# A hybrid decoder step: the first pair of expert blocks gathered before the last row tile is routed, its rows added by products with a selection matrix

## Chip, cores and metric

One core of a Trainium2 chip runs the whole program as one launch. The metric is the device time of that launch in microseconds.

## What is computed

One trunk layer for 512 prompt tokens and 8 samples, 520 rows of 1024, all in fp32. A mixer (pooling and a state-space scan) is followed by the output projection and a residual. Then comes the part that matters here, a mixture of 32 experts, cut to its core:

```python
def _hier_moe(u, ...):
    t = u.reshape(n * L, d)                      # u = rmsnorm(h)
    g_w, g_idx = lax.top_k(softmax(t @ rg_w + rg_b), 1)      # one group of 4
    e_w, e_idx = lax.top_k(softmax(e_sel), 2)                # two of its 8 experts
    hg = einsum('td,edf->tef', t, w_gate[g]); hu = einsum('td,edf->tef', t, w_up[g])
    act = silu(hg) * hu * gate[:, :, None]
    out = out + einsum('tef,efd->td', act, w_down[g])
```

After it come a gated per-layer input and a last norm. Each token has two experts, 1040 choices in all.

## The kernel before

The kernel is written engine by engine; the order on each engine is written out by hand, and semaphores join them. Names: `pe` is TensorE, `dve` VectorE, `act` ScalarE, `pool` GpSimd, `sp` SyncE, which only issues DMA.

**Row tiles.** The 520 rows are five tiles, taken in the order `ORDER = [0, 1, 4, 2, 3]` (tile 4 holds the 8 samples, tile 3 comes last). For each, `out_half` makes the output projection, `residual` (VectorE) adds it into `h1`, `half_square` and `inverse_root` make 1/rms on ScalarE and GpSimd, and `store_row` (ScalarE) writes the normed rows to the DRAM buffer `u_dram`. In parallel `h_rows` transposes h, `take_h` copies it with the gain, `route` makes the router's logits, and on VectorE `take_logits`, `choose` and `rank` pick two experts for each row (one-hot in `oh`) and the row's place among the rows of its expert; the count behind `rank` is a product (`count`) of triangular and full ones with the choices so far. `rank` leaves `posh`, for each row the one-hot of its place times its token number.

**Blocks.** An expert's rows fill a block of 64 places; two blocks make a pair of 128. `fill_slots(i)` multiplies `posh` by the choices and sums, over all five tiles, the table of row numbers for the 16 pairs of the first 32 blocks (bank PS[1]); VectorE turns it into `out_all` and `idx_all`. A place with no row keeps the number EMPTY and falls out of the gather's bounds, so G, cleared before, holds zeros there. `fill_extra_slots` does the same for blocks beyond the first 32.

**The hand-over.** GpSimd waits for the table and for all five stores of `u_dram`, then gathers pairs 0 and 1 into the two halves of `G` (an indirect DMA each). `pair_rows` transposes G's rows by TensorE, four tiles for each half of the 1024 features, and `take_pair` copies them with the gain to `uT`. Every later pair is gathered two pairs ahead.

**The expert blocks.** Block b on TensorE: `gate_up` (16 products for gate and up from `uT`), `down` of block b-1, half a pair's `pair_rows`, then `act_rows`, which transposes the activations. ScalarE makes silu, VectorE `gate_act`, `take_pair` and `take_act`. The first 24 blocks are written out (`HEAD`), the rest are a loop whose length VectorE computes (`extra_blocks`). SyncE loads 3 MB of weights for each block; there are seven buffers for gate and up and five for down. Those of blocks 0, 1, 3 and 6 are loaded early, those of 2, 4 and 5 when the output projection is done, and block b+7 when `gate_up(b)` is done:

```python
for b in range(HEAD):
    if b >= 1:
        ...
        sp.wait_ge(s_Y_ready, b)          # down(b - 1) done
        load_down(dn_slot(nxt), bass.ds(nxt, 1))
    if b + NGU < HEAD + U:
        sp.wait_ge(s_up_done, b + 1)      # gate_up(b) done
        load_gate_up(gu_slot(b + NGU), bass.ds(b + NGU, 1))
```

Behind the blocks come the scatter of the last rows, their loads by token, the gate of the per-layer input and the last norm.

Of the kernel before, what the change touches and what calls it, by code (L numbers as in the profile page):

```python
# [12 lines left out]
BF16 = mybir.dt.bfloat16  # L13
I32 = mybir.dt.int32
U32 = mybir.dt.uint32
ALU = mybir.AluOpType
# [88 lines left out]
def build(nc, a, o):  # L105
    ctx = ExitStack()
    with ctx:
# [77 lines left out]
        junk = at(R_g, D)  # L185
        spool = at(R_act, PW, rows=NS * BUF)
# [189 lines left out]
        s_slot_ready = sem("s_slot_ready")  # L376
        s_pos_ready = sem("s_pos_ready")
# [87 lines left out]
        def _(sp):  # L465
# [28 lines left out]
            sp.dma_start(o["conv_s"][0, :, 0:2, :], a["state_conv"][0, :, 1:3, :]).then_inc(st_shift, 16)  # L494

# [90 lines left out]
            sp.wait_ge(st_shift, 32)  # L586
# [4 lines left out]
        def _(pe):  # L591
# [314 lines left out]
            def fill_slots(i):  # L906

                pe.wait_ge(s_pos_ready, i + 1)
                for k in range(2):
                    j = 2 * ORDER[i] + k  # L910
                    choice = oh[:, ORDER[i], k * NE:(k + 1) * NE].rearrange("p (b q) -> p q b", q=2)
                    for q in range(2):
                        ins = pe.matmul(PS[1][q * S:(q + 1) * S, 0:MAIN], posh[:, j, :], choice[:, q, :],
                                        start=(i == 0 and k == 0), stop=(i == NT - 1 and k == 1))
# [3 lines left out]
            def fill_extra_slots():  # L918
                pe.wait_ge(s_slot_ready, 1)
                for j in range(2 * NT):  # L920
                    for q in range(2):
                        ins = pe.matmul(PS[3][q * S:(q + 1) * S, MAIN:NP_], posh[:, j, :],
                                        blkx[:, j, :].rearrange("p (b q) -> p q b", q=2)[:, q, :],
                                        start=(j == 0), stop=(j == 2 * NT - 1))
                ins.then_inc(s_tab_done, 1)
# [181 lines left out]
        def _(act):  # L1107
# [144 lines left out]
            def half_square(i, h):  # L1252
# [3 lines left out]
                squares = A(junk[0:R, h * 512:(h + 1) * 512], h1[0:R, t, h * 512:(h + 1) * 512], ACT.Square, scale=root_d,  # L1256
# [8 lines left out]
            def store_row(i):  # L1265
# [6 lines left out]
                act.wait_ge(s_u_ready, i + 1)  # L1272
                act.dma_start(u_dram[t * P:t * P + R, :], row[0:R, i % 2, :]).then_inc(u_stored[i % 2], 16)
# [22 lines left out]
            for b in range(HEAD):  # L1296
                act.wait_ge(s_up_done, b + 1)
                silu_gate(b)
                if b >= 1:
                    act.wait_ge(s_Y_ready, b)  # L1300
                    if b % 2 and b >= 5:
                        act.wait_ge(y_written[(b // 2) % 2], 16 * (b // 4))
# [87 lines left out]
        def _(pool):  # L1390
# [71 lines left out]
            pool.wait_ge(st_fin, 16)  # L1462
            for i in range(NT):
# [23 lines left out]
            for p in range(2):  # L1487
                gather(p, idx_all[:, p:p + 1])
# [40 lines left out]
        def _(dve):  # L1529
# [228 lines left out]
            def rank(i):  # L1758
# [7 lines left out]
                for k in range(2):  # L1766
# [4 lines left out]

            residual(0, 0)
# [35 lines left out]
            residual(4, 1)  # L1808
            take_h(4, 1)
# [3 lines left out]

            dve.wait_ge(s_tab_done, 1)
            step(ts(out_all[:, 0:MAIN], PS[1][:, 0:MAIN], float(EMPTY), None, ALU.add))
            ts(idx_all[:, 0:MAIN], out_all[:, 0:MAIN], 1, None, ALU.arith_shift_right).then_inc(s_tab_ready, 1)

            step(tt(ex4, L[:, :, 0:4], gmax[:, :, 0:1].to_broadcast((P, NT, 4)), ALU.subtract))
            tt(e21, ev[:, :, 1], ev[:, :, 0], ALU.subtract).then_inc(s_rt_a, 1)

# [12 lines left out]
            step(dve.tensor_copy(rank_i, rk))  # L1833
            step(ts(rank_i, rank_i, 6, None, ALU.arith_shift_right))
            step(dve.tensor_copy(rq, rank_i))
            step(stt(rr, rq, -float(S), rk, ALU.mult, ALU.add))

            step(ts(cmp0, rq, 0.5, None, ALU.is_gt))
            step(tt(ovt, ovt, rq, ALU.add))
            step(tt(ovt, ovt, cmp0, ALU.mult))  # L1840
            step(ts(ovt, ovt, -1.0, None, ALU.add))

            tt(posh, iota_s.unsqueeze(1).to_broadcast((P, 2 * NT, S)),
               rr.rearrange("p t k -> p (t k)").unsqueeze(2).to_broadcast((P, 2 * NT, S)), ALU.is_equal)
            step(tt(blkx, iota_s[:, 0:NBX].unsqueeze(1).to_broadcast((P, 2 * NT, NBX)),
                    ovt.rearrange("p t k -> p (t k)").unsqueeze(2).to_broadcast((P, 2 * NT, NBX)), ALU.is_equal))
            tt(blkx, blkx, const[:, C_TOKID:C_TOKID + 2 * NT].unsqueeze(2).to_broadcast((P, 2 * NT, NBX)), ALU.mult
               ).then_inc(s_slot_ready, 1)

            dve.wait_ge(s_rt_b, 1)  # L1850
            step(dve.tensor_reduce(gw, ex4, AX.X, ALU.add))
            step(stt(gw, e21, 1.0, gw, ALU.add, ALU.mult))
            step(dve.reciprocal(wgt[:, :, 0], gw))
            step(tt(wgt[:, :, 1], wgt[:, :, 0], e21, ALU.mult))

            def extra_blocks():
                dve.wait_ge(s_tab_done, 2)
# [16 lines left out]
            def take_pair(slot, half):  # L1874
                tt(uT[:, slot, half * 512:half * 512 + 512].rearrange("p (k c) -> p k c", c=P), tiles(PS[6 + half][:, :]),  # L1875
# [177 lines left out]
```

## Time and profile before

| | |
|---|---|
| median of 3 runs | 575.98 us (574.41 to 576.43) |
| the profiled execution: its time, its span | 574.31 us, 572.5 us |
| TensorE busy, share of the span | 509.9 us, 89% |
| VectorE, ScalarE, GpSimd busy | 207.7, 153.7, 110.7 us |
| bytes moved by DMA, mean rate | 144.72 MB, 253 GB/s |
| mean granted TensorE clock | 0.961 |

A fp32 product is recorded as two instructions, a transpose as one. The hand-over lies at 218 to 249 us of the span, the expert blocks from there to 488, the tail behind them. The share of busy time is a mean over stages with different limits; which wait ends last has to be read stage by stage.

### The profile page before, as it was taken

What the parts mean: (1) busy time and instruction counts of PE and PEld (TensorE: products, weight loads), DVE (VectorE), ACT (ScalarE), POOL (GpSimd) and SP (SyncE); (2) the same over time, 40 slices, a digit from 0 to 9 for tenths busy, and PEclk for the clock granted to TensorE, in tenths of its full rate; (3) what the DMA queues carried; (4) which work ended last, traced back from release to release, by engine and by line L of the source; (5) the groups of instructions that cost most, each with busy time, mean ns of one, the idle gap of its engine ahead of it and who ended that gap; (6) DMA issues with size and microseconds to landing.
All of it is one profiled execution on the core that took longest, in us unless ns stands there. A gap on an engine that the chain in (4) does not pass through costs nothing.

```text
span 572.5 us, 7815 instructions
## 1 busy us (share of the span) xinstructions
PE 509.9 (89%) x3098; PEld 313.3 (55%) x3098; DVE 207.7 (36%) x496; ACT 153.7 (27%) x315; POOL 110.7 (19%) x178
## 2 busy tenths in 40 slices
PE   5899999999999995299999999978849999799994
PEld 4788886768645553255555555534424553344443
DVE  1285696322034456431112221111111110467455
ACT  0435263113424022012222222221111223433224
POOL 1200059991001001201111111101111222111001
PEclk9999999999999998589999999998987999899998
DMA  8990002303359506849999999999999998700001
GB/s 289 417 291 2 1 1 73 149 1 89 147 243 395 246 37 258 330 174 393 419 416 415 414 416 417 415 416 418 416 406 384 410 412 344 306 2 2 38 37 73
DMA packets 40214, 144.72 MB, mean 253 GB/s; under 512 B 14522, under 2 KB 15162, under 8 KB 31076
## 3 DMA queue, kind: packets, MB, share of 16 engines
q1 hardware_dynamic: 33316, 132.79, 58.6%
q0 software_dynamic: 5152, 8.85, 4.2%
q10 hardware_dynamic: 1712, 2.62, 1.2%
q8 instruction: 23, 0.38, 0.3%
q14 instruction: 11, 0.09, 0.0%
HBM read 140.15 MB, written 14.19 MB: 270 GB/s over the span
## 4 chain that ended last, share of the span: by engine, by line
PE 45%; DMA 10%; DVE 3%; issue 2%; ACT 1%; SPq 0%; POOL 0%; POOLq 0%; DVEq 0%; ACTq 0%
PE PS L989 18%; PE PS L1091 10%; PE PS L1010 10%; DMA mem<-in_exp_w_down 5%; PE PS L593 4%; DVE mem L1875 2%; DMA u_rows<-mem 2%; DMA mem<-u_rows,idx_all 1%; DMA choice_rows<-mem,out_i 1%; PE PS L834 1%; PE PS L935 1%; PE PS L990 1%; DMA mem<-choice_rows 1%; DVE mem L1917 1%; PE PS L996 1%
## 5 line engine op out<-in xcount | busy, mean ns | idle before, releaser
L989 PE MATMUL PS<-mem 128*64 128x256 f32 x512 | 119.6, 387 | 6.8 <-DVE mem L1875 6.8
L990 PE MATMUL PS<-mem 128*64 128x256 f32 x512 | 119.6, 387 | 0.0
L989 PEld LDWEIGHTS PS<-mem 128*64 128x64 f32 x512 | 68.6, 139 | 43.3 <-DVE mem L1875 7.6
L1010 PE MATMUL PS<-mem 128*64 128x512 f32 x256 | 64.2, 624 | 16.8 <-DMA mem<-in_exp_w_down 8.6
L633 PE MATMUL PS<-mem 128*128 128x260 f32 x320 | 73.3, 385 | 0.0
L990 PEld LDWEIGHTS PS<-mem 128*64 128x64 f32 x512 | 68.6, 139 | 0.0
L633 PEld LDWEIGHTS PS<-mem 128*128 128x128 f32 x320 | 59.8, 190 | 10.5 <-issue 1.5
L593 PEld LDWEIGHTS PS<-mem 128*128 128x128 f32 (+4 forms) x254 | 31.7, 172 | 47.8 <-issue 30.6
L1879 DVE TENSOR_TENSOR mem<-PS,mem 64x256 f32<-64x256 f32 x32 | 13.7, 427 | 120.0 <-ACT mem L1288 120.0
L821 PE MATMUL PS<-mem 128*128 128x512 f32 x128 | 56.6, 595 | 0.0
L1091 PE MATMUL PS<-mem 128*128 128x512 f32 (+1 forms) x144 | 55.6, 545 | 0.0
L593 PE MATMUL PS<-mem 128*128 128x128 f32 (+4 forms) x254 | 40.6, 292 | 14.7 <-DMA mem<-u_rows,idx_all 12.4
L1875 DVE TENSOR_TENSOR mem<-PS,mem 128x512 f32<-128x512 f32 x34 | 23.5, 692 | 75.4 <-PE PS L593 75.2
L1288 ACT ACTIVATE mem<-PS 64x256 f32<-64x256 f32 x32 | 12.0, 376 | 134.8 <-PE PS L990 134.8
L1010 PEld LDWEIGHTS PS<-mem 128*64 128x64 f32 x256 | 18.8, 141 | 42.6 <-issue 30.6
L1091 PEld LDWEIGHTS PS<-mem 128*128 128x128 f32 x144 | 27.1, 190 | 26.6 <-issue 25.8
L1402 POOL TENSOR_TENSOR mem<-mem 128x1 f32<-128x1 f32 (+1 forms) x20 | 4.1, 207 | 182.0 <-ACT mem L1256 85.1
L821 PEld LDWEIGHTS PS<-mem 128*128 128x128 f32 x128 | 23.8, 190 | 26.9 <-issue 26.8
L604 PE MATMUL PS<-mem 128*128 128x260 f32 x128 | 31.3, 410 | 6.9 <-DMA mem<-in_w_a 6.9
L1293 ACT ACTIVATE mem<-PS 64x512 f32<-64x512 f32 x32 | 18.9, 591 | 65.4 <-PE PS L1010 65.4
L604 PEld LDWEIGHTS PS<-mem 128*128 128x128 f32 x128 | 26.1, 205 | 11.3 <-DMA mem<-in_w_a 6.9
L1480 POOL DMA_INDIRECT mem<-u_rows,idx_all x15 | 15.3, 1022 | 81.5 <-PE PS L593 72.6
(270 smaller groups left out, 546.8 us busy)
## 6 DMA issues: line engine op xcount, KB each, us to landing
mem<-in_exp_w_down SPq DMA_DIRECT2D x32, 1024.0 KB, 21.2
mem<-in_exp_w_gate SPq DMA_DIRECT2D x32, 1024.0 KB, 18.7
mem<-in_exp_w_up SPq DMA_DIRECT2D x32, 1024.0 KB, 21.9
mem<-in_w_out SPq DMA_DIRECT2D x2, 2048.0 KB, 7.5
mem<-in_ple_gate_w SPq DMA_DIRECT2D x1, 4096.0 KB, 29.6
mem<-choice_rows SPq DMA_DIRECT2D x4, 1024.0 KB, 8.4
mem<-in_xT SPq DMA_DIRECT2D x4, 520.0 KB, 9.1
mem<-in_w_a SPq DMA_DIRECT2D x4, 512.0 KB, 9.9
```

The source lines that it names most:

```text
L593: return pe.transpose(dst, src, ident[0:n, 0:n])
L604: ins = pe.matmul(PS[A_BANKS[j][h]][:, 0:HALF], COLS[j][2][:, k, :], xg[k // 4][:, k % 4, h * HALF:(h + 1) * HALF], start=(k == 0), stop=( ...
L633: ins = pe.matmul(PS[b + h][:, 0:HALF], w[:, k, :], aT[:, k, h * HALF:(h + 1) * HALF], start=(k == 0), stop=(k == KT - 1))
L821: return pe.matmul(PS[OUT_BANKS[i][h]][:, :], mix_col(k, ORDER[i]), w_out[:, k, h * 512:(h + 1) * 512], start=(k == 0), stop=(k == KT - 1))
L989: pe.matmul(PS[0][0:S, 0:FF], rows_k, gu[slot][:, k, :], start=(k == 0), stop=(k == KT - 1))
L990: ins = pe.matmul(PS[1][S:2 * S, 0:FF], rows_k, gu[slot][:, KT + k, :], start=(k == 0), stop=(k == KT - 1))
L1010: ins = pe.matmul(PS[4 + h][h * S:(h + 1) * S, :], actT[:, s % 2, f * S:(f + 1) * S], dn[slot][:, f, h * 512:(h + 1) * 512], start=(f == 0 ...
L1091: ins = pe.matmul(PS[4 if q else 2 * (i % 2) + h][:, 0:w], uTr[:, i % 2, k * P:(k + 1) * P], w_ple[:, k, h * 512 + q * w:h * 512 + (q + 1) ...
L1293: A(ysb[rows, s // 2, 0:512], PS[4][0:S, :], ACT.Copy)
L1480: pool.indirect_dma_start(G[:, q, :], None, u_dram, bass.IndirectOffsetOnAxis(ap=idx, axis=0), bounds_check=TOK - 1, oob_is_err=False).the ...
L1875: tt(uT[:, slot, half * 512:half * 512 + 512].rearrange("p (k c) -> p k c", c=P), tiles(PS[6 + half][:, :]), g_ffn[:, 4 * half:4 * half + ...
L1879: tt(act_tok[:, s % 2, :], PS[1][S:2 * S, 0:FF], sg[:, s % 2, :], ALU.mult).then_inc(s_act_ready, 1)
```

## The change

The table of the first pair is summed once more, apart, over the first four tiles in order (`first_pair_slots`, two columns, PS[1]), and pair 0 is gathered from it as soon as these four tiles are stored. Rows of the last tile (tile 3) are missing in G then, and stay zero there. VectorE builds from the last tile's ranks and choices a selection matrix `sel` of 128 rows by 128 places, with the row's 1/rms as its value (`first_pair_rows`). TensorE sums, in two cleared banks, eight products of G's rows with the identity and eight of the raw `h1` of the last tile with `sel` (`first_pair`); the sum is what the transposed rows were. The full table moves to PS[3] and is made afterwards; pair 1 is gathered with it, once its half of G, where `sel` and its parts are kept until then, has been cleared.

The extra slots, both halves of pair 1's transposes and `extra_blocks` move behind the down product of block 0, in block 1's turn; VectorE's `extra_choices` (overflow ranks and weights) moves behind block 0's gate. ScalarE squares into another scratch (`junk_h`). The DRAM rows of the last tile are first filled with a copy of `x_prompt`, issued early on SyncE, the last store waits for it.

```diff
+            sp.dma_start(u_dram[tl * P:(tl + 1) * P, :], a["x_prompt"][0, tl * P:(tl + 1) * P, :]).then_inc(st_shift, 16)
...
+            SEL = [PS[0], PS[2]]
+            def first_pair_zero():
+                pe.wait_ge(s_outp_out, 9)
+                for half in range(2):
+                    pe.matmul(SEL[half][:, :], bef[:, 0:1].to_broadcast((P, P)), const[:, 0:256].bitcast(BF16),
+                              start=True, stop=False)
+            def first_pair(rows, place, half, last_part):
+                for q in range(4):
+                    ins = pe.matmul(SEL[half][:, q * P:(q + 1) * P], rows.rearrange("s (p k) -> s k p", k=KT)[:, 4 * half + q, :],
+                                    place, start=False, stop=last_part and q == 3)
+                if last_part:
+                    ins.then_inc(s_T_done, 1)
+            def first_pair_slots():
+                pe.wait_ge(s_pos_ready, NT - 1)
+                for i in range(NT - 1):
+                    for k in range(2):
+                        t = ORDER[i]
+                        choice = oh[:, t, k * NE:(k + 1) * NE].rearrange("p (b q) -> p q b", q=2)
+                        for q in range(2):
+                            ins = pe.matmul(PS[1][q * S:(q + 1) * S, 0:2], posh[:, 2 * t + k, :], choice[:, q, 0:2],
+                                            start=(i == 0 and k == 0), stop=(i == NT - 2 and k == 1))
                 ins.then_inc(s_tab_done, 1)
...
             out_half(4, 1, 6, KT)
+            first_pair_slots()
             h_rows(4, 1)
             route(4)
+            first_pair_zero()
             for i in range(NT - 1):
                 fill_slots(i)
             count(4)
+            pe.wait_ge(g_full[0], 16)
+            for half in range(2):
+                first_pair(G[:, 0, :], ident, half, False)
+            pe.wait_ge(s_sel_ready, 1)
+            for half in range(2):
+                first_pair(h1[:, ORDER[NT - 1], :], sel, half, True)
             fill_slots(4)
             count_all()
...
-            pe.wait_ge(g_full[0], 16)
-            pe.wait_ge(s_lg_out, NT)
-            pair_rows(0, 0)
-            pe.wait_ge(s_cnt_taken, 1)
-            pair_rows(0, 1)
-            fill_extra_slots()
...
-                if b % 2 == 0:
-                    pe.wait_ge(g_full[(b // 2 + 1) % 2], 16 * ((b // 2 + 1) // 2 + 1))
-                pair_rows((b // 2 + 1) % 2, b % 2)
+                if b == 1:
+                    pe.wait_ge(g_full[1], 16)
+                    pe.wait_ge(s_lg_out, NT)
+                    pe.wait_ge(s_cnt_taken, 1)
+                    pair_rows(1, 0)
+                    pair_rows(1, 1)
+                    fill_extra_slots()
+                elif b >= 2:
+                    if b % 2 == 0:
+                        pe.wait_ge(g_full[(b // 2 + 1) % 2], 16 * ((b // 2 + 1) // 2 + 1))
+                    pair_rows((b // 2 + 1) % 2, b % 2)
...
             pool.wait_ge(st_fin, 16)
+            step(pool.memset(G[:, 0, :], 0.0))
...
-            step(pool.memset(G, 0.0))
-
-            pool.wait_ge(s_tab_ready, 1)
-            pool.wait_ge(u_stored[0], 48)
-            pool.wait_ge(u_stored[1], 32)
...
-            for p in range(2):
-                gather(p, idx_all[:, p:p + 1])
+            pool.wait_ge(s_tab_ready, 1)
+            pool.wait_ge(u_stored[0], 32)
+            pool.wait_ge(u_stored[1], 32)
+            pool.wait_ge(st_shift, 48)
+            gather(0, idx_i[0][:, 0:1])
+            pool.wait_ge(s_T_done, 2)
+            step(pool.memset(G[:, 1, :], 0.0))
+            pool.wait_ge(s_tab_ready, 2)
+            pool.wait_ge(u_stored[0], 48)
+            gather(1, idx_all[:, 1:2])
...
+            def first_pair_rows(i):
+                t = ORDER[i]
+                R = ROWS[t]
+                step(tt(hit[0:R], iota_s[0:R, :].unsqueeze(1).to_broadcast((R, 2, S)),
+                        rk[0:R, t, :].unsqueeze(2).to_broadcast((R, 2, S)), ALU.is_equal))
+                for k in range(2):
+                    ins = stt(selk[0:R, k], hit[0:R, k].unsqueeze(1).to_broadcast((R, 2, S)), rstd[0:R, 5 + t:6 + t],
+                              oh[0:R, t, k * NE:k * NE + 2].unsqueeze(2).to_broadcast((R, 2, S)), ALU.mult, ALU.mult)
+                step(ins)
+                tt(sel[0:R, :].rearrange("p (q s) -> p q s", s=S), selk[0:R, 0], selk[0:R, 1], ALU.add).then_inc(s_sel_ready, 1)
...
             residual(4, 1)
+            dve.wait_ge(s_tab_done, 1)
+            step(ts(out_i[0][:, :], PS[1][:, 0:1], float(EMPTY), None, ALU.add))
+            ts(idx_i[0][:, :], out_i[0][:, :], 1, None, ALU.arith_shift_right).then_inc(s_tab_ready, 1)
             take_h(4, 1)
             take_logits(4)
             choose(4)
             rank(4)
...
+            first_pair_rows(4)
...
+            for half in range(2):
+                dve.wait_ge(s_T_done, half + 1)
+                take_rows_of(PS[2 * half], 0, half)
+
+            dve.wait_ge(s_tab_done, 2)
...
             for b in range(HEAD):
                 dve.wait_ge(s_sg_ready, b + 1)
                 gate_act(b)
-                dve.wait_ge(s_T_done, b + 3)
-                take_pair((b // 2 + 1) % 2, b % 2)
+                if b == 0:
+                    extra_choices()
+                else:
+                    for n in (range(2) if b == 1 else range(b % 2, b % 2 + 1)):
+                        dve.wait_ge(s_T_done, 2 * (b // 2) + 3 + n)
+                        take_pair((b // 2 + 1) % 2, n)
                 dve.wait_ge(s_actT_done, b + 1)
                 take_act(b)
-                if b == 0:
+                if b == 1:
                     extra_blocks()
```

## Rows read from the trace of the kernel before

**Rows 1.** The chain that ended last, 215 to 262: start us, us, what.

```profile
221.63 8.84 DMA u_rows<-mem
...
231.50 7.76 DMA mem<-u_rows,idx_all
...
239.30 1.97 PE PS L593 x8
...
241.27 2.25 PE PS L922 x40
...
244.03 0.42 PE PS L989
...
249.34 0.39 ACT mem L1288
```

**Rows 2.** Timeline of TensorE: start us, us, engine, line, tiles, shapes, count.

```profile
210.06 1.88 PE L886 MATMUL PS<-mem 128*128 128x40 f32 x16
...
216.02 1.96 PE L821 MATMUL PS<-mem 128*128 128x512 f32 x4
...
218.76 0.66 PE L593 MATMUL PS<-mem 128*128 128x128 f32 x4 [0.78 <-DVE mem L1710]
...
221.29 1.11 PE L913 MATMUL PS<-mem 128*64 128x16 f32 x32
...
239.30 1.97 PE L593 MATMUL PS<-mem 128*128 128x128 f32 x8 [12.45 <-DMA mem<-u_rows,idx_all]
```

**Rows 3.** Stretches: length, busy of each engine, then TensorE clock, DMA share, GB/s.

```profile
220.00:224.00 4.00, 2.37 (x43) 2.10 (x42) 2.40 (x14) 1.15 (x1) 2.12 (x2) 1.00 1.00 412
...
240.00:244.00 4.00, 4.00 (x50) 3.48 (x51) 1.38 (x2) 0.00 (x0) 0.99 (x1) 0.50 0.16 43
...
248.00:252.00 4.00, 3.70 (x32) 2.34 (x30) 2.15 (x7) 0.38 (x1) 0.00 (x0) 1.00 0.35 109
...
424.00:428.00 4.00, 0.00 (x0) 0.00 (x0) 0.00 (x0) 0.00 (x0) 0.00 (x0) 0.69 0.99 396
```

**Rows 4.** Timeline of SyncE's queue, its DMA issues.

```profile
39.81 0.64 SPq L494 DMA_DIRECT2D out_conv_s<-in_state_conv  x1
...
249.34 0.33 SPq L484 DMA_DIRECT2D mem<-in_exp_w_gate  x1
...
255.93 0.38 SPq L490 DMA_DIRECT2D mem<-in_exp_w_down  x1
```

**Rows 5.** Waits of TensorE, 360 to 480: in total, times, longest.

```profile
PE PS L1010 <- DMA mem<-in_exp_w_down: 8.6, 2, 7.4
```

**Rows 6.** Timeline of VectorE, 226 to 234.

```profile
226.65 0.17 DVE L1815 TENSOR_SCALAR out_all<-PS 128x16 int32<-128x16 f32 x1 [0.71 <-PE PS L913]
...
228.79 0.49 DVE L1831 TENSOR_TENSOR mem<-mem 128x320 f32<-128x320 f32 x1
...
229.85 0.17 DVE L1833 CAST int_w<-mem 128x10 int32<-128x10 f32 x1
...
233.65 0.17 DVE L1854 TENSOR_TENSOR mem<-mem 128x5 f32<-128x5 f32 x1
```

**Rows 7.** Timeline of GpSimd, ahead of the first gather.

```profile
220.31 1.80 POOL L1467 MEMSET mem<- 128x2048 f32 x1
```

**Rows 8.** Single transfers, by line: one load of weights (L490), one gather (L1480).

```profile
L490 SPq DMA_DIRECT2D mem<-in_exp_w_down x1: 447/447/447, 221.0 to 221.0; - x1
...
DMA to landing us min/median/max: 21.0/21.0/21.0
...
L1480 POOL DMA_INDIRECT mem<-u_rows,idx_all x1: 988/988/988, 242.0 to 242.0; - x1
...
DMA to landing us min/median/max: 3.9/3.9/3.9
```

**Rows 9.** Stretches around TensorE's restart at 430, columns as in rows 3.

```profile
430.00:432.00 2.00, 1.67 (x4) 0.53 (x6) 0.00 (x0) 0.00 (x0) 0.00 (x0) 0.50 0.89 363
...
435.00:436.00 1.00, 1.00 (x7) 0.93 (x8) 0.69 (x1) 0.34 (x1) 0.44 (x3) 0.63 1.00 336
```

More of the change, by code:

```diff
@@ L185, in build @@
         junk = at(R_g, D)
+        junk_h = at(R_g + D, D)
+        sel = at(R_g + D, 2 * S)
+        selk = at(R_g + D + 2 * S, 2, 2, S)
+        hit = at(R_g + D + 6 * S, 2, S)
         spool = at(R_act, PW, rows=NS * BUF)
@@ L376, in build @@
         s_slot_ready = sem("s_slot_ready")
+        s_sel_ready = sem("s_sel_ready")
         s_pos_ready = sem("s_pos_ready")
@@ L912, in fill_slots @@
                     for q in range(2):
-                        ins = pe.matmul(PS[1][q * S:(q + 1) * S, 0:MAIN], posh[:, j, :], choice[:, q, :],
+                        ins = pe.matmul(PS[3][q * S:(q + 1) * S, 0:MAIN], posh[:, j, :], choice[:, q, :],
                                         start=(i == 0 and k == 0), stop=(i == NT - 1 and k == 1))
@@ L1272, in store_row @@
                 act.wait_ge(s_u_ready, i + 1)
+                if i == NT - 1:
+                    act.wait_ge(st_shift, 48)
                 act.dma_start(u_dram[t * P:t * P + R, :], row[0:R, i % 2, :]).then_inc(u_stored[i % 2], 16)
@@ L1300, in _ @@
                     act.wait_ge(s_Y_ready, b)
+                    if b == 1:
+                        act.wait_ge(u_stored[0], 48)
+                        act.wait_ge(u_stored[1], 32)
                     if b % 2 and b >= 5:
@@ L1812, in _, with take_rows_of @@
             rank(4)
-            dve.wait_ge(s_tab_done, 1)
-            step(ts(out_all[:, 0:MAIN], PS[1][:, 0:MAIN], float(EMPTY), None, ALU.add))
-            ts(idx_all[:, 0:MAIN], out_all[:, 0:MAIN], 1, None, ALU.arith_shift_right).then_inc(s_tab_ready, 1)
+            first_pair_rows(4)
             step(tt(ex4, L[:, :, 0:4], gmax[:, :, 0:1].to_broadcast((P, NT, 4)), ALU.subtract))
             tt(e21, ev[:, :, 1], ev[:, :, 0], ALU.subtract).then_inc(s_rt_a, 1)
+            def take_rows_of(bank, slot, half):
+                tt(uT[:, slot, half * 512:half * 512 + 512].rearrange("p (k c) -> p k c", c=P), tiles(bank[:, :]),
+                   g_ffn[:, 4 * half:4 * half + 4].unsqueeze(2).to_broadcast((P, 4, P)), ALU.mult).then_inc(s_uT_ready, 1)
+            for half in range(2):
+                dve.wait_ge(s_T_done, half + 1)
+                take_rows_of(PS[2 * half], 0, half)
+            dve.wait_ge(s_tab_done, 2)
+            step(ts(out_all[:, 0:MAIN], PS[3][:, 0:MAIN], float(EMPTY), None, ALU.add))
+            ts(idx_all[:, 0:MAIN], out_all[:, 0:MAIN], 1, None, ALU.arith_shift_right).then_inc(s_tab_ready, 1)
             oh4 = oh.rearrange("p t (k e) -> p (t k) e", e=NE)
@@ L1843, in _ @@
[L1843 to L1848, printed above, removed]
@@ L1874, in take_pair @@
             def take_pair(slot, half):
-                tt(uT[:, slot, half * 512:half * 512 + 512].rearrange("p (k c) -> p k c", c=P), tiles(PS[6 + half][:, :]),
-                   g_ffn[:, 4 * half:4 * half + 4].unsqueeze(2).to_broadcast((P, 4, P)), ALU.mult).then_inc(s_uT_ready, 1)
+                take_rows_of(PS[6 + half], slot, half)
             def gate_act(s):
@@ L1882, in take_act @@
                 dve.tensor_copy(actT[:, s % 2, :], PS[2][:, 0:2 * S]).then_inc(s_actT_ready, 1)
-            for half in range(2):
-                dve.wait_ge(s_T_done, half + 1)
-                take_pair(0, half)
             for b in range(HEAD):
```

42 lines of the change are left out of this document (26 added, 16 removed).

## The prediction

> **What bounds the kernel now.** I read the chain that ended last first, around the hand-over from routing to the expert blocks. From 221.63 to 249.3 us it is one string of five pieces: the store of the last row tile (8.84 us), the gather of the first pair of blocks (7.76), eight transposes of its rows (1.97), the extra-slot products (2.25), then the sixteen gate/up products of block 0, 5.8 us up to ScalarE's first gate at 249.34 [rows 1]. TensorE has nothing to do from 226.84 to 239.30 [rows 2].
>
> Next the stage behind it, since a gain here is worth only what the block stage lets through. The windows show the weight stream: the prefetch of blocks 2, 4 and 5 fills the DMA engines until about 240, then their share is 0.16 at 240 to 244, still 0.35 at 248 to 252, and behind that, but for one short gap, about 1.0, as still at 424 to 428 [rows 3]. SyncE can refill no slot before block 0's products end: refill A goes out at 249.34, refill B waits for block 0's down product and goes out at 255.93 [rows 4]. Past 360, the down products wait 8.6 us for their weights in the records, and longer than that in all [rows 5]. So the blocks are bound by the weight stream, and the stream's start is set by the end of block 0. What brings that end forward brings the whole stream forward, as long as it falls into the idle stretch 240 to 250. The stages behind the blocks then follow rigidly.
>
> **The change part by part.** I compare when block 0's gate/up products end: 249.3 before.
>
> *The gather leaves earlier.* It left at 231.50, 1.03 us after the store of the last tile landed [rows 1]. Now it needs the slot table of four tiles only. The last out projection products end at 217.98; 16 small products for 2 columns cost what the 16 for 16 columns did (32 instructions, 1.11 us) [rows 2], and the two VectorE conversions take 0.38 (0.17 each and the gap, [rows 6]), so the table is there at 219.6. GpSimd comes later: its fifth inverse root ends as the 1.80 us clearing of G starts, at 220.3, and that clearing is gone (half to before the roots, where GpSimd idles, half to behind the sums) [rows 7]. With the idle step and an issue of some 0.7 us: 221.1, **10.4 us earlier**. The stores it waits for are long done.
>
> *How long it takes.* It starts as the 7 MB prefetch fills the queues; the last of its seven loads goes out at 221.04 [rows 8]. Near rows: 7.76 us for this gather, 8.84 for the store issued at 221.63, both beside the prefetch [rows 1]; 3.9 for a gather at 242.04 on quiet DMA [rows 8]. Full queues are the nearer case: 7.8 us, it lands at 228.9. **0**, with ends -3.9 and +1.1. The Trainium skill, "DMA: Bandwidth & Descriptors", section "Anatomy of one DMA — SWDGE (gpsimd) path", fits 2.0 us plus bytes / 436e3 per microsecond for a DMA from GpSimd; for some 65 rows of 4 KB that gives an estimate of 2.6 us. Both loaded rows here disagree threefold; by the fit the sum would be some 4 us better (the quick-gather rival).
>
> *Sixteen products for eight transposes.* A transpose is one instruction, an fp32 product two. At full clock four transposes take 0.66 us and 16 instructions of 128x128 weights with 40 columns 1.88, each with the tail of the last [rows 2]: about 0.11 us apiece, so I price a product of 128 columns at two of those. At half clock it is 0.22: double that, and the eight transposes in 1.97 with the tail of the last agree [rows 1]. The clock was at half, 1.2 of 2.4 GHz, after TensorE's idle time, at 240 to 244 [rows 3], and will be again, since TensorE is idle from some 225.2 to 228.9. When it took up dense products at 430.33 after a wait (busy 1.67 of the first two us), the clock was back within the slice 435 to 436, 5.3 us later [rows 9]. So of 32 x 0.22 = 7.0 us, 5.3 run at half and the rest in 0.85; with 0.15 for the tail, 6.3 us: **4.3 more** than the 1.97. Bounds: all at full 3.7, all at half 7.2.
>
> The Trainium skill, "TensorE: Matmul & The Clock Gate", section "Terms", calls the transpose mode four times faster for fp32. No row here has a transpose and a product of the same 128 columns side by side; by this rule a product would cost four transposes and sixteen of them 14.1 us (a rival below).
>
> *The selection matrix must not be late.* The table products delay the last transposes of h by 0.35 us (218.76 to 219.1, [rows 2]), the conversions fit before them, so the last rank ends at 226.3 instead of 225.94. Four VectorE operations of 128 elements follow; between 0.17 for 16 and 0.49 for 320 [rows 6] I put 0.28 each, 1.25 with gaps: ready at 227.5. It is wanted only after the first eight products, at some 232.4. Cost **0**; the cover is 5 us. The two clearing products (bf16, 512 columns, some 0.5 us in all) lie in TensorE's wait for the last choice.
>
> *Between products and block 0.* The 2.25 us of extra-slot products leave the path. In their place stands VectorE's last copy, 0.85 with its start; the last slot fill and the total count (some 0.9 together at half clock) lie beside it. **-1.4**. They return behind block 1's down product at full clock, some 1.35 us.
>
> *Block 0 at full clock.* Before, the clock was back only for the slice from 248 [rows 3], with a pair of products every 0.42 us until then [rows 1]. Now it starts 7 us after TensorE resumed, at full clock, 3.6 us: **-2.2**, with 0 as the other end.
>
> *Block 0's down product.* VectorE now works out the overflow (4.0 us, 229.85 to 233.82 in [rows 6]) between block 0's gate and the copy of its activation. Gate/up of block 1 (3.6) covers most; 0.35 us of wait is left: **+0.35**. The second gather can't leave until G's second half, which holds the matrix, is cleared: 0.9 us after the sums, at about 237; at 7.8 us it lands at 245, before the down product ends at 246.6. A tail of only 1.6 us, so I give it +0.5 in the range. Queued behind that wait are both row transposes of pair 1, the extra slots and block 1's activation, so block 2 and refill C.
>
> *The stream.* A moves by -9.7, B by -9.35, block 2 by only some -7.5 (both halves of pair 1 and the extra slots now sit in front of it). B to C grows from 6.8 to 8 us; B's 3.1 MB and two row transfers need about 8.2, so at most a gap of some 0.2 opens. Behind that the stream is full and the 1.9 us by which TensorE lags is taken from its own waits past 360. The 0.5 MB copy in DRAM is issued on SyncE at 40.5, behind the copy at 39.81, where SyncE has nothing else to issue for long after [rows 4]: 0. ScalarE's added waits find their transfers done. The other scratch area costs nothing.
>
> Sum: -10.4 + 0 + 4.3 - 1.4 - 2.2 + 0.35 + 0.2 = **-9.2 us**. Against the profiled execution's 574.31 that is 565.1; that execution is 1.7 below the median of the runs, so against 575.98 it is **566.8**. A change under 0.5% (2.9 us) can't be told from none here.
>
> **The rivals.**
> *The clock stays low.* If all products run at half, 0.9 is lost; if block 0 does too (sixteen pairs at 0.42, [rows 1]), 3.2 more: 567.7 to 570.9. For it: before, TensorE worked from 239.3 and the clock was back only at 248 [rows 3]. Against: most of that was transposes and 12-column products; the dense ones began at 243.5.
>
> *Quick gather.* It leaves two or three microseconds into the prefetch and takes the 3.9 us of quiet DMA [rows 8]: lands at 225, the first eight products are done when the matrix comes, the sums end 3.7 earlier, 563.1. Against: the share is 1.00 from 220 on [rows 3].
>
> *Products at four times a transpose.* 14.1 for 6.3 us: -1.4 remains, 575.4 with the clock as above; no measurable change.
>
> *The stream hides it.* If the blocks are bound by bytes and the idle share at 240 to 252 isn't usable, TensorE only waits longer past 360: 576. Against it, refill A starts the stream within 2 us.
>
> *Slower: the gather is held in the burst.* It now shares the engines with the prefetch's start, no longer with its end. If its rows come through only as the burst drains, it lands when the last prefetch does, 21.0 us after that one's issue at 221.04 [rows 8], at 242.0. That is 13.1 later than I count: +3.9, 579.9. It decides from a landing at 238.1 on, where the 9.2 are used up. Against: the store issued at 221.63 beside the same burst took 8.84.
>
> **How the numbers follow.** As summed 0.50 (own range 564.5 to 568.5); clock stays low 0.20; quick gather 0.10; four-fold products 0.05; stream hides it 0.06; held gather 0.06; 0.03 for something else on the good side. Faster by over 0.5%: 0.83, within 0.11, slower 0.06. The range must hold 8 in 10: from just under the quick gather, 563.0, to the low clock with 1.3 us of bounds on the gather, 572.5.
>
> **What would show it.** Right: first gather leaves at 221 to 222 and lands near 229; 32 instructions with 128-column weights from there in about 6 us, the last part at 1.0 clock; matrix ready before the first half of them is through; ScalarE's first gate near 239.6; refill A there; no DMA share under 0.9 after some 249; the wait before the down products past 360 as before or a bit shorter. Wrong: a landing past 235, products over 0.3 us per instruction, TensorE waiting for the second gather, or a start 9 us earlier that is gone at 430, when the block loop begins.

## The result and the profile after

| | before | after |
|---|---|---|
| median of six runs each | 575.84 us (573.72 to 576.89) | 571.5 us (569.77 to 572.77) |
| profiled execution: time, span | 574.31, 572.5 us | 571.64, 569.8 us |
| mean granted clock | 0.961 | 0.971 |

The ratio is 0.9911, with a 95% interval of 0.9883 to 0.9939: 5.1 us less by the ratio, between 3.5 and 6.7; the two medians alone lie 4.3 us apart. That is faster, as forecast, and 571.5 lies in the range of 563.0 to 572.5, near its slow end. The gain is about half of the 9.2 us of the point.

The chain that ended last, after, has three pieces where before had five [rows 1]: the gather, the products, then VectorE's copy and block 0.

```profile
222.40 10.35 DMA mem<-u_rows,idx_i
232.79 7.92 PE PS L946 x32
240.73 0.70 DVE mem L1888
241.47 0.43 PE PS L1033
...
245.20 0.38 ACT mem L1336
```

No store stands in front of the gather any more. Its 10.35 us and the 7.92 of the products (L946) are both longer than forecast (7.8 and 6.3). ScalarE's first gate comes at 245.20 instead of 249.34 [rows 1].

TensorE's timeline, after:

```profile
217.66 1.96 PE L828 MATMUL PS<-mem 128*128 128x512 f32 x4
219.55 1.10 PE L959 MATMUL PS<-mem 128*64 128x2 f32 x32
...
232.79 7.90 PE L946 MATMUL PS<-mem 128*128 128x128 f32 x32 [5.64 <-DMA mem<-u_rows,idx_i]
...
246.16 0.34 PE L1040 MATMUL PS<-mem 64*128 64x64 f32 x2 [1.01 <-DVE mem L1957]
...
250.46 1.94 PE L1054 MATMUL PS<-mem 128*64 128x512 f32 x8 [0.36 <-DVE mem L1960]
252.33 1.16 PE L600 MATMUL PS<-mem 128*128 128x128 f32 x8
```

The first row ends the output projection at 219.62; before it ended at 217.98 [rows 2]. So this execution was 1.64 us late before the change had done anything on the path. One place shows where, a stretch of the mixer far ahead of the routing, columns as in rows 3:

```profile
28.00:32.00 4.00, 4.00 (x13) 3.15 (x12) 3.96 (x12) 1.52 (x2) 0.00 (x0) 0.58 0.99 410
```

TensorE's clock was 0.58 there and 1.00 before, at the same work. Such a dip is in the profiles of five experiments below (0.50 to 0.72) and missing in three; one of the five, the kernel before with the copy alone, has the median of the kernel before. So it isn't put down to the change. Nor can the copy of the prompt's rows have caused it: SyncE issues it at 40.24 here and at 40.31 in the kernel with the copy alone, behind the dip. All comparisons of this stage therefore count from the end of the output projection, or from the first load behind it.

Counted so, the first gate moved by 5.8 us (from 31.4 to 25.6 us behind the output projection). The profiled times differ by only 2.7 us: of the 5.2 us found below, 1.65 went in the late start and 0.9 behind the blocks, where the clock was at half for some 7 us of the tail's start, and for 3.4 before.

Stretches, after:

```profile
240.00:244.00 4.00, 3.78 (x40) 2.74 (x42) 2.96 (x12) 0.00 (x0) 2.08 (x3) 1.00 0.26 104
244.00:248.00 4.00, 2.99 (x30) 1.75 (x28) 2.23 (x11) 0.38 (x1) 0.88 (x1) 1.00 0.76 230
248.00:252.00 4.00, 3.63 (x28) 1.62 (x24) 2.67 (x9) 0.38 (x1) 0.00 (x0) 1.00 0.98 403
252.00:256.00 4.00, 4.00 (x62) 3.17 (x62) 2.16 (x7) 1.18 (x2) 0.99 (x1) 1.00 0.70 214
```

The DMA share at 240 to 244 is 0.26, between the end of the prefetch and refill A, and 0.70 at 252 to 256, before refill B comes through. Before it was 0.16 and, as late as 248 to 252, 0.35 [rows 3]. The clock is at 1.00 in all four; before it was at 0.50 at 240 [rows 3].

Where the clock had fallen, after:

```profile
222.00:223.00 1.00, 0.97 (x7) 0.91 (x7) 0.03 (x1) 0.92 (x1) 0.76 (x3) 0.77 0.98 410
223.00:224.00 1.00, 0.78 (x5) 0.59 (x5) 0.25 (x1) 0.23 (x1) 0.59 (x1) 0.50 1.07 434
```

It went to half at some 222.5, in a slice in which TensorE was busy for 0.97 us, and TensorE's pause began only at 227.14. In the kernel with the gather behind the last store (below) it fell at 221.0, between two slices busy for 0.97 and 1.00. So the low clock that the products met was there before the pause; the prediction had it come from the idle time.

SyncE's queue, after: refills A and B.

```profile
245.19 0.33 SPq L489 DMA_DIRECT2D mem<-in_exp_w_gate  x1
...
252.44 0.38 SPq L495 DMA_DIRECT2D mem<-in_exp_w_down  x1
```

The chain further on, after, and TensorE's waits from 360 to 480:

```profile
400.35 26.35 DMA mem<-in_exp_w_down
```

```profile
PE PS L1054 <- DMA mem<-in_exp_w_down: 8.6, 2, 7.4
PE PS L1054 <- issue: 8.0, 5, 2.5
```

The recorded wait for down weights is 8.6 us as before [rows 5]. The long transfer at 400.35 lands at 426.70, and with it TensorE is released for the last stretch of the blocks. I call this landing the release: it is the one number that tells what the start of the stream is worth.

### The profile page after: what moved, and what is told of

It reads as the page before. It is cut to its first block, busy times and chain, and to the rows that moved or that the text cites. A ratio compares the mean times of both kernels' runs of the same rounds, so it can differ in the third digit from the quotient of the medians.

```text
span 569.8 us, 7942 instructions
## 1 busy us (share of the span) xinstructions
PE 515.1 (90%) x3155; PEld 319.6 (56%) x3156; DVE 209.2 (37%) x502; ACT 153.6 (27%) x315; POOL 111.0 (19%) x179
## 4 chain that ended last, share of the span: by engine, by line
PE 45%; DMA 8%; DVE 4%; issue 2%; SPq 1%; ACT 0%; POOL 0%; POOLq 0%; DVEq 0%; ACTq 0%
PE PS L1033 17%; PE PS L1137 10%; PE PS L1054 9%; DMA mem<-in_exp_w_down 5%; PE PS L600 4%; DVE mem L1888 2%; DMA mem<-u_rows,idx_i 2%; PE PS L946 1%; DMA choice_rows<-mem,out_i 1%; PE PS L841 1%; SPq L489 1%; PE PS L971 1%; DMA mem<-choice_rows 1%; PE PS L1034 1%; DVE mem L1995 1%
## 5 line engine op out<-in xcount | busy, mean ns | idle before, releaser
L1033 PE MATMUL PS<-mem 128*64 128x256 f32 x512 | 117.3, 382 | 6.7 <-DVE mem L1888 6.7
L1034 PE MATMUL PS<-mem 128*64 128x256 f32 x512 | 117.4, 382 | 0.0
L1033 PEld LDWEIGHTS PS<-mem 128*64 128x64 f32 x512 | 67.5, 137 | 42.0 <-DVE mem L1888 7.6
L1054 PE MATMUL PS<-mem 128*64 128x512 f32 x256 | 62.6, 610 | 17.6 <-DMA mem<-in_exp_w_down 8.6
L1034 PEld LDWEIGHTS PS<-mem 128*64 128x64 f32 x512 | 67.5, 137 | 0.0
L640 PEld LDWEIGHTS PS<-mem 128*128 128x128 f32 x320 | 59.8, 190 | 10.5 <-issue 1.5
L600 PEld LDWEIGHTS PS<-mem 128*128 128x128 f32 (+4 forms) x246 | 30.1, 170 | 32.8 <-issue 29.4
L1054 PEld LDWEIGHTS PS<-mem 128*64 128x64 f32 x256 | 18.3, 139 | 43.2 <-issue 30.4
L600 PE MATMUL PS<-mem 128*128 128x128 f32 (+4 forms) x246 | 38.3, 287 | 1.8 <-DVE mem L1995 1.8
L1527 POOL DMA_INDIRECT mem<-u_rows,idx_all x14 | 14.1, 1009 | 67.3 <-PE PS L600 66.2
```

What stands on the lines that cost most here:

```text
L600: return pe.transpose(dst, src, ident[0:n, 0:n])
L640: ins = pe.matmul(PS[b + h][:, 0:HALF], w[:, k, :], aT[:, k, h * HALF:(h + 1) * HALF], start=(k == 0), stop=(k == KT - 1))
L1033: pe.matmul(PS[0][0:S, 0:FF], rows_k, gu[slot][:, k, :], start=(k == 0), stop=(k == KT - 1))
L1034: ins = pe.matmul(PS[1][S:2 * S, 0:FF], rows_k, gu[slot][:, KT + k, :], start=(k == 0), stop=(k == KT - 1))
L1054: ins = pe.matmul(PS[4 + h][h * S:(h + 1) * S, :], actT[:, s % 2, f * S:(f + 1) * S], dn[slot][:, f, h * 512:(h + 1) * 512], start=(f == 0 ...
L1527: pool.indirect_dma_start(G[:, q, :], None, u_dram, bass.IndirectOffsetOnAxis(ap=idx, axis=0), bounds_check=TOK - 1, oob_is_err=False).the ...
```

## The experiments

Two questions: which of the two long terms ate the gain, and by what rule does time won at the first gate turn into time at the end? For the second, every kernel's stream is measured alike. All times count from the issue of the first prefetch load of the kernel. "Idle" is the sum of 1 minus the DMA share over 48 slices of 1 us, those whose share is under 0.93; the first slice starts 1.5 us behind that issue, when the loads have begun to move. Ratios are against the kernel before, run on the same chip; a gain that the text takes from a ratio is that ratio times 576.

| kernel | first gate | DMA idle | release | median, ratio (interval) |
|---|---|---|---|---|
| before | 31.3 | 10.95 | 212.3 | |
| after | 25.6 | 5.6 | 207.05 | 571.5, 0.9911 (0.9883 to 0.9939) |
| matrix products first | 21.75 | 2.4 | 203.2 | 566.34, 0.9842 (0.9808 to 0.9877) |
| loads behind the gather | 12.4 | 0.3 | 199.0 | 569.72, 0.9903 (0.9873 to 0.9934) |
| gather behind the last store | 33.6 | 13.8 | 215.2 | 578.84, 1.0048 (1.0023 to 1.0073) |
| plain weights | 23.55 | 3.35 | 205.9 | 570.02, 0.9891 (0.9859 to 0.9922) |
| refill held | 25.4 | 10.7 | 211.7 | 575.83, 0.9976 (0.9949 to 1.0003) |
| more products | 25.7 | 5.7 | 206.9 | 570.95, 0.9898 (0.9868 to 0.9927) |
| copy alone | 31.5 | 11.2 | 212.5 | 576.81, 1.0003 (0.9976 to 1.0029) |
| stream filled | 21.9 | 1.5 | 202.9 | 566.57, 0.9826 (0.979 to 0.9862) |

### Matrix products first

The eight products with the selection matrix open the sum, those of G's rows close it:

```diff
-            pe.wait_ge(g_full[0], 16)
-            for half in range(2):
-                first_pair(G[:, 0, :], ident, half, False)
             pe.wait_ge(s_sel_ready, 1)
             for half in range(2):
-                first_pair(h1[:, ORDER[NT - 1], :], sel, half, True)
+                first_pair(h1[:, ORDER[NT - 1], :], sel, half, False)
+            pe.wait_ge(g_full[0], 16)
+            for half in range(2):
+                first_pair(G[:, 0, :], ident, half, True)
```

> The changed kernel with the two groups of first-pair products exchanged: the eight with the selection matrix first, the eight with G's rows behind the wait for the gather. Theory A (the products are paid one by one at 0.25 us an instruction, and only those behind the landing of the gather are on the path): the matrix group runs in the wait, the sums end 4.0 us after the landing instead of 7.9, block 0's first gate comes 3.9 us earlier against the landing, and as the weight stream starts with it the time falls by 3.5 to 4 us from 571.5, to about 567.8. Theory B (once the gather has landed the stream is full anyway and the start no longer decides): no change from 571.5. The gather's own duration stays at about 10 us in both.

566.34 us, by the ratio 9.1 us under before (7.1 to 11.1), and better than the 567.8 of theory A. TensorE's timeline in this kernel:

```profile
227.36 7.91 PE L946 MATMUL PS<-mem 128*128 128x128 f32 x32 [2.32 <-DVE mem L1837]
```

The products wait for the matrix (L1837) and run through without a break: when the first 16 instructions were done, at 231.3, the gather, issued at 220.77 and 10.4 us under way, had just landed. Some half of the products lie beside the gather, and the first gate comes 3.8 us earlier than after. The release moved by the same 3.8. In the changed kernel the matrix was there 3.4 us before the gather, as VectorE's timeline of it shows:

```profile
229.12 0.29 DVE L1837 TENSOR_TENSOR mem<-mem 128x128 f32<-128x128 f32 x1
```

So the order in the change puts the work that could start at 229.4 behind the work that can't start before 232.8. The remaining 0.4 of the 3.8 us come from the matrix itself, which was there 9.3 us behind the output projection and 9.8 after: the last routing products (L893) took 2.10 us there and 2.57 after, where the clock fell among them. In this kernel the first products wait for the matrix and not for the gather, so a faster gather alone would win nothing more.

### Loads behind the gather

SyncE issues the prefetch of blocks 2, 4 and 5 only when the first gather has landed:

```diff
             sp.wait_ge(s_outp_done, 2 * NT)
+            sp.wait_ge(g_full[0], 16)
             load_gate_up(gu_slot(2), bass.ds(2, 1))
```

> The changed kernel, with the seven prefetch loads (blocks 2, 4 and 5) held until the first gather has landed. Theory A (the gather took 10.35 us because it shares the DMA engines with that burst): it takes about 4 us, as the gather issued onto quiet DMA did before, the products start 6 us earlier, block 0's gate comes some 4 us earlier (the matrix, ready at 229.4, then holds the second group back); the prefetch starts 6 to 7 us later and ends at about 243 to 244, beyond block 0's end, so that the stream gains less: 568 to 571. Theory B (10 us is what this gather takes, whatever is beside it): it still takes 10, the prefetch is 11 us late, and the time rises to 575 or more.

Its chain and, behind it, one stretch:

```profile
220.67 5.26 DMA mem<-u_rows,idx_i
...
225.97 7.92 PE PS L947 x32
```

```profile
218.00:222.00 4.00, 3.96 (x61) 3.41 (x60) 2.04 (x6) 1.87 (x3) 2.09 (x4) 1.00 0.02 4
```

Without the prefetch the gather takes 5.26 us instead of 10.35: the prefetch's start costs it 5.1. The store of the last tile still ran beside it. The first gate comes at 238.4 us of the span, against 245.2 after (243.6 with the late start taken off). Yet the time is that of the changed kernel, within the 568 to 571 of theory A, since the DMA engines stood nearly still at 218 to 222 (share 0.02) and had only the gather and the store until the loads went out at 226.00. Counted from the end of the output projection, the release is at 207.1 us in both kernels. What the gather won, the stream lost.

### Gather behind the last store

```diff
             pool.wait_ge(st_shift, 48)
+            pool.wait_ge(u_stored[0], 48)
             gather(0, idx_i[0][:, 0:1])
```

> The changed kernel, but the first gather also waits for the store of the last row tile, as it did before the change; all else stays. It tells what the early gather alone is worth inside the change. Theory A: the gather leaves at 231.5 to 233 instead of 222.4 and lands near 240.5, block 0's gate comes at 252 to 253, and the time is some 2 to 3 us above the kernel before (578 to 579): the products and the moved work alone are a loss. Theory B (the early gather isn't what brought the gain; moving the extra slots behind block 0 did): below 575.

```profile
221.59 8.79 DMA u_rows<-mem
...
231.32 7.79 DMA mem<-u_rows,idx_i
...
239.16 7.94 PE PS L946 x32
```

With the gather back behind the store (its chain, above), store and gather take what they took before, 8.79 and 7.79 against 8.84 and 7.76 [rows 1], and the kernel is by the ratio 2.8 us slower than before (1.3 to 4.2), as theory A had it. That is the change without its early gather: the products cost more than all that it saves elsewhere. The first gate is 2.3 us later than before, idle 2.8 more, the release 3.0 later.

### Plain weights

The products read each 128 features side by side instead of every eighth. Pair 0 then has its features in another order than its weights, so the kernel computes something else and only its times are of use:

```diff
-                    ins = pe.matmul(SEL[half][:, q * P:(q + 1) * P], rows.rearrange("s (p k) -> s k p", k=KT)[:, 4 * half + q, :],
+                    ins = pe.matmul(SEL[half][:, q * P:(q + 1) * P], rows.rearrange("s (k p) -> s k p", k=KT)[:, 4 * half + q, :],
```

> The changed kernel, with the rows in the first-pair products taken as 128 neighbouring features per weight load instead of every eighth one. This changes which features blocks 0 and 1 get, so part of the computation differs; count and shape of all instructions are the same. Theory A (the products cost twice my price because their weights are read with a stride of 32 bytes): weight loads of these products fall from 336 ns to the 190 ns of the other fp32 loads and the 32 instructions from 7.9 us to about 4 to 5; block 0's gate comes 3 us earlier. Theory B (an fp32 product whose weights are 128 columns and whose moving side is 128 costs 0.25 us an instruction whatever the layout): 7.9 us as before.

The weight loads of the products, first in the changed kernel, then in this one (ns shortest/median/longest):

```profile
L946 PEld LDWEIGHTS PS<-mem x32: 312/336/339, 232.8 to 240.2; 128*128 128x128 f32 x32
```

```profile
L946 PEld LDWEIGHTS PS<-mem x32: 192/333/333, 234.5 to 239.9; 128*128 128x128 f32 x32
...
234.54 5.71 PE L946 MATMUL PS<-mem 128*128 128x128 f32 x32 [6.32 <-DMA mem<-u_rows,idx_i]
```

And two stretches of this kernel:

```profile
236.00:238.00 2.00, 2.00 (x11) 2.00 (x11) 0.00 (x0) 0.00 (x0) 0.00 (x0) 0.50 1.01 426
238.00:240.00 2.00, 2.00 (x18) 2.00 (x17) 0.61 (x1) 0.00 (x0) 0.00 (x0) 0.88 0.98 416
```

The products take 5.7 us for 7.9, more than the 4 to 5 of theory A, since only the part at full clock gets shorter: there 13 loads begin within 1.4 us, some 0.12 us for each. At half clock a load takes some 333 ns in both, at full clock 192 here and still 336 with every eighth feature. So with the strided rows the products don't quicken when the clock does; in the changed kernel it was back at 236 (this slice had 0.50 before):

```profile
236.00:237.00 1.00, 1.00 (x7) 1.00 (x5) 0.00 (x0) 0.00 (x0) 0.00 (x0) 0.91 0.97 410
```

and yet the second 16 instructions took as long as the first, 0.247 us each. The release comes 1.2 us earlier than after. The two ratios (0.9891 against 0.9911) can't tell so little. The first gate comes 2.0 us earlier, not 3.

### Refill held, and more products

Two kernels ask by what rule the gain reaches the end. In the first, SyncE holds refill A until block 0's down product is done; TensorE's work stays. In the second, block 9, deep in the full stream, gets four more products of 512 columns into a bank that nobody reads then.

```diff
                 if b + NGU < HEAD + U:
+                    if b == 0:
+                        sp.wait_ge(s_Y_ready, 1)
                     sp.wait_ge(s_up_done, b + 1)
```

> The changed kernel, but SyncE issues the first refill (gate and up weights of block 7) only when block 0's down product is done, 7.3 us after the gate/up products that free the buffer; nothing on TensorE changes. Theory A (the start of the weight stream sets the end): the DMA engines stay idle through the stretch in which this refill ran (5 us of transfer), the stream ends 5 us later, and the time rises by about 5 us to 576 to 577, with TensorE's longer wait only past 350. Theory B (TensorE's own start sets the end): no change, 571.5, since block 7's weights still come long before block 7.

```diff
+                if b == 9:
+                    for _ in range(4):
+                        pe.matmul(PS[3][:, :], ident, h1[:, 0, 0:512], start=True, stop=True)
```

> The changed kernel with four more fp32 products of 512 columns in block 9 (eight instructions, 3.4 us on TensorE, into a bank that nothing reads); the stream's start is untouched. Theory A (the blocks are bound by the stream): the 3.4 us come out of TensorE's own waits past 360, no change from 571.5. Theory B (TensorE sets the end): 575.

The held refill, in its SyncE queue and in a stretch:

```profile
252.28 0.33 SPq L489 DMA_DIRECT2D mem<-in_exp_w_gate  x1
```

```profile
248.00:252.00 4.00, 3.63 (x26) 1.49 (x22) 2.51 (x9) 0.38 (x1) 0.00 (x0) 1.00 0.00 0
```

The first gate is where it was (25.4), the stream is idle 5.1 us longer, the release is 4.7 us later, and 575.83 us is 4.3 above the changed kernel's median (3.7 by the two ratios), a little under the 5 of theory A. The added products, in its TensorE timeline and waits:

```profile
305.43 3.70 PE L1078 MATMUL PS<-mem 128*128 128x512 f32 x8
```

```profile
PE PS L1054 <- issue: 4.8, 3, 1.7
```

3.70 us of TensorE's time cost nothing: the release is at 206.9, and 3.2 us are gone from the waits recorded as issue (8.0 after). Here the stream sets the time and TensorE doesn't.

### Copy alone

The kernel before with only the copy of the prompt's rows and the wait for it:

```diff
+            tl = ORDER[NT - 1]
+            sp.dma_start(u_dram[tl * P:(tl + 1) * P, :], a["x_prompt"][0, tl * P:(tl + 1) * P, :]).then_inc(st_shift, 16)
...
+                if i == NT - 1:
+                    act.wait_ge(st_shift, 48)
```

> The kernel before, with only the early copy of the last tile's rows from DRAM to DRAM added, and the last store waiting for it. Theory A (the copy runs in idle stretches and costs nothing): 576.0, within 1 us of the kernel before. Theory B (the 1.6 us by which the changed kernel's profiled execution was late at 218 us come from this copy): 577.5.

Ratio 1.0003 (0.9976 to 1.0029): the copy costs nothing. Its profile has the dip at 28 to 32 us (0.57), and the first three experiments, which have the copy too, don't.

### Stream filled

The matrix products first, and two moves for refill B: SyncE issues block 8's gate and up weights ahead of block 5's down weights, and VectorE copies block 0's activation before the overflow.

```diff
+                if b == 1:
+                    sp.wait_ge(s_up_done, 2)
+                    load_gate_up(gu_slot(1 + NGU), bass.ds(1 + NGU, 1))
...
                 take_act(b)
+                if b == 0:
+                    extra_choices()
```

> The kernel with the matrix group first, and two orders more. SyncE issues block 8's gate and up weights as soon as block 1's gate/up products are done, ahead of the wait for block 0's down product (behind which stands block 5's down weight); VectorE copies block 0's activation before it works out the overflow. Theory A (the stream's idle stretch of 2 us between the first two refills is paid in full at the end): that stretch closes, and the time falls from 566.3 to about 564.5. Theory B (only the first refill's start counts): 566.0 to 566.3.

566.57 us, what the matrix-first kernel has. The forecast 564.5 didn't come, but theory A wasn't tested either: the idle time fell only from 2.4 to 1.5 us. Its stretches say where the rest sits:

```profile
240.00:244.00 4.00, 2.99 (x28) 1.75 (x26) 1.93 (x8) 0.38 (x1) 1.03 (x2) 1.00 0.89 319
...
252.00:256.00 4.00, 4.00 (x32) 1.96 (x28) 2.61 (x11) 0.38 (x1) 0.00 (x0) 1.00 1.01 412
256.00:260.00 4.00, 4.00 (x36) 2.73 (x36) 0.89 (x2) 1.18 (x2) 1.01 (x1) 1.00 0.81 284
```

The gap of refill B went to the third refill, at 256 to 260. The release is 0.3 us earlier, which is under what the runs can tell. The matrix-first kernel stays the simplest of the best.

## Why the prediction was right and where it was off

Each step by what it measured, from the output projection's end to the first gate:

| step | forecast | measured |
|---|---|---|
| the gather leaves earlier | -10.4 | -10.7 |
| how long it takes | 0 (-3.9 to +1.1) | +2.6 |
| sixteen products for eight transposes | +4.3 | +5.95 |
| between products and block 0 | -1.4 | -1.5 |
| block 0 at full clock | -2.2 | -2.1 |
| first gate | -9.7 | -5.8 |

**Two terms were mis-sized**, together by 4.2 us, and the first gate missed by 3.9. The mechanism, a hand-over without the last store on its path, was right. That 571.5 still lies in the range is in part luck: the range's slow end was made of a clock that stays low and 1.3 us on the gather. Block 0 ran at full clock, and the two errors that did occur both went beyond the bounds given for them.

*How long it takes* failed first, and its upper bound with it. I took 7.8 us from the gather and the store that ran beside the prefetch's second half, and let a new start inside the burst be only 1.1 worse. The gather now leaves 2.8 us after the first prefetch load and takes 10.35 us, 10.54 in the plain-weights kernel; put back behind the store it takes 7.79, and without the prefetch 5.26. In all six kernels that issue it there it takes 10.2 to 10.5. So its cost goes with how much of the burst is still ahead of it. One rival isn't separated: the last tile's store now runs beside the gather and didn't before. Without the burst, but beside that store, the gather took 5.26, against 3.9 to 4.0 for gathers on quiet queues, so up to some 1.3 of the 2.6 us may be the store's. The held gather, as a rival, had the mechanism right and the size wrong: it lands 13.1 us behind the first load, not with the last one. The quick gather wasn't there; even the prefetch's absence gave 5.26 and not 3.9. The Trainium skill's page "DMA: Bandwidth & Descriptors", section "Anatomy of one DMA — SWDGE (gpsimd) path", by which I had estimated 2.6 us, is met by none of these gathers.

*Sixteen products* failed in its upper bound too: 7.2 us for "all at half" is less than the 7.92 measured. The clock came back 3.4 us after TensorE resumed, and I had taken 5.3 from the restart at 430. That error should have helped and didn't: with the gather behind the store the clock took 5.7 us to come back, and the products took 7.94. What I had wrong was the price: two transposes for a product, at each clock. At half clock that was nearly right (0.44 us for 0.49), at full it was under half (0.22 for 0.49). The transposes of the same strided rows run eight in 1.16 us at full clock, a product's two instructions take 0.49, so a product is here nearly four transposes' worth once their tail is taken off. The rival of four-fold products had this ratio, but put it on the half-clock transpose as well and so came to 14.1 us. (Its time was summed wrongly too: with -1.4 us left it is 574.6, not 575.4.) The plain-weights kernel, which changes the layout alone, shows what the pace goes with: loading the strided weights, 336 ns whatever the clock. Read side by side, a product costs some 0.23 us at full clock, close to my price of 0.22. The rule it was weighed by (the Trainium skill, "TensorE: Matmul & The Clock Gate", section "Terms") agrees with this case at full clock and with strided weights. At half clock a strided product costs about 2.2 transposes, and one with plain weights at full clock about 1.8, so the agreement is one of this layout.

*The matrix* was ready 9.8 us behind the output projection (forecast 9.5), under its cover and never late. But the cover was the wrong thing to look at: I checked that it wasn't late and not whether it was early. It was 3.4 us early, and that is most of what the swapped order wins.

*The clock stays low* didn't happen; all of block 0 ran at 1.00. *Block 0's down product* waited 0.36 us (0.35 forecast). The second gather left at 242.57 and landed 4.0 later on quiet queues, well before 252.33, where TensorE wants it, so it made no wait.

*The stream.* That the whole stream comes forward "as long as it falls into the idle stretch" held, and the table makes it sharper. Release minus idle is 201.3 us before, 201.5 after, and between 200.8 and 201.5 in all kernels but two: plain weights, 202.5, and loads behind the gather, 198.7, where store and gather no longer lie between the loads (some 1.9 us by my estimate, 0.8 MB at 412 GB/s). So the time for which the DMA engines stand still behind the first prefetch load is paid at the end, to within about 1 us: with slices laid from the issue itself, idle is 0.7 to 1.5 more and the same difference is 199.3 to 200.6. Refill held shows that this is a cause and doesn't only go along: same TensorE, more idle time, the gain nearly gone. More products shows the reverse. *The stream hides it* is refuted by the same pair, since the idle stretch was worth 4 us when taken away. The gap between A and B is the size forecast in issue (7.25 us for 7.0). Its idle stretch, a share of 0.70 at 252 to 256 and so 1.2 us, isn't new: before, the share at 256 to 260 was 0.70 too. The sum's +0.2 was for a gap between B and C, which are 7.95 us apart (forecast 8); none opened, the share at 256 to 260 is 1.04.

From gate to result: the first gate moved by 5.8 us, idle fell by 5.4, the release by 5.2, and the time by 5.1 (by the ratio). In the other kernels the release and the time by the ratio move together too, to within 0.8 us: with the matrix products first the release moves by 9.1, and so does the time. For the loads behind the gather this holds only from the end of the output projection, as said there.

**Still open.** Why the clock dips at 28 to 32 in some executions, and what takes the clock down while TensorE is busy, how much of the gather's 2.6 us is the store's, and why the plain-weights kernel's release comes 1.1 us later behind its idle time than the others'. No run was made of plain weights and swapped order together; by the table it could win at most the last microseconds of idle time, 2.4.

## What to carry to other kernels

When a sum is split so that part of it can start before a transfer lands, put first the part whose inputs are there first; compare the ready times, not only whether the later one has cover. In front of a stretch bound by a stream of bytes, count the time in which the stream stands still, since that is what comes back at the end. TensorE's own time is free there until it opens such a gap: 3.70 us in block 9 cost nothing. A small transfer that is on the path should be priced at the moment it enters a burst, not from one that ran near the burst's end: here 10.4 against 7.8 us, and 5.3 without it.

## What the hardware showed that was not expected

- Loading fp32 weights from rows read at every eighth element took 336 ns at either level of the clock, side by side 333 ns at 1.2 GHz and 192 at 2.4. In the first-pair products, a product of 128 columns so costs 0.49 us, whatever the clock.
- The gather of one pair took 3.9 to 4.0 us on quiet queues (a later pair), 5.26 beside one store, 7.8 late in the burst of loads and 10.2 to 10.5 early in it, beside the store.
- TensorE's clock fell to half while TensorE was busy (0.97 us of the slice at 222), 4.6 us before its pause. It was back at full 3.4 us after the same products began, 3.2 and 5.7 us in the kernels with the matrix first and with the gather behind the store; the restart at 430 had taken 5.3 us [rows 9].
- Four fp32 products of 512 columns, 3.70 us, vanished in the waits of the block stage.
